# Attention stage of a one-core encoder layer: finished rows stored from SyncE, and the order of transposes, products and closings changed

## The reference, cut to what matters

```
def fox_attend(q, k, v, cq, ck, pos_q, pos_k):
    s = einsum('bqhd,bkhd->bhqk', q, k) * HEAD_DIM ** -0.5          # float32
    decay = cq[..., :, None] - ck[..., None, :]
    s = where(pos_k <= pos_q, s + decay, NEG_INF)
    p = softmax(s, axis=-1)
    return einsum('bhqk,bkhd->bqhd', p, v)
```

## Time and profile before

| | us |
|---|---|
| median of 3 runs | 2924.09 (2922.81 to 2926.6) |
| the profiled execution, its own time | 2925.41 |
| its span | 2923.8 |
| attention, from the span's start | about 640 to 1169 |
| PE busy over the span | 2766.0 (95%) |
| DVE, ACT, POOL busy | 1271.9, 895.1, 927.0 |
| mean granted TensorE clock | 0.978 |

### The profile page before, as it was taken

One profiled execution on the slowest core, in us unless ns is written; L12 is line 12 of the kernel. 1 busy time (PEld: TensorE's weight loads), 2 busy tenths in 40 slices (PEclk: granted clock), 3 DMA queues, 4 the chain that ended last, 5 costly groups with the idle time before them and its releaser, 6 DMA issues.

```text
span 2923.8 us, 40223 instructions
## 1 busy us (share of the span) xinstructions
PE 2766.0 (95%) x14550; PEld 2424.5 (83%) x14550; DVE 1271.9 (44%) x2362; ACT 895.1 (31%) x1621; POOL 927.0 (32%) x613
## 2 busy tenths in 40 slices
PE   7999999999898988799699999999999999999997
PEld 6899899987777777588599999999987888888886
DVE  4333343348786777577423223232235223222235
ACT  3201201127676766455211111212122121121122
POOL 3233334211111111444233333333245333333333
PEclk9999999999999999899899999999999999999999
DMA  6543535674433333566910111111146111111113
GB/s 180 183 125 116 159 104 157 197 186 120 104 94 93 94 93 94 164 210 208 259 57 30 57 43 43 43 43 43 43 130 197 59 44 48 53 43 56 44 43 115
DMA packets 261442, 305.23 MB, mean 104 GB/s; under 512 B 19324, under 2 KB 221704, under 8 KB 256712
## 3 DMA queue, kind: packets, MB, share of 16 engines
q1 hardware_dynamic: 209272, 256.14, 29.6%
q0 software_dynamic: 14304, 21.63, 2.9%
q10 hardware_dynamic: 37744, 25.96, 2.8%
HBM read 221.21 MB, written 82.21 MB: 104 GB/s over the span
## 4 chain that ended last, share of the span: by engine, by line
PE 46%; DMA 2%; POOL 2%; DVE 1%; ACT 0%; issue 0%; SPq 0%; POOLq 0%
PE up_bank L2340 23%; PE dn_bank L2363 23%; DMA m_x_in<-scratch_x 1%; DVE y L2294 1%; POOL y L2158 1%; DMA m_h_lo<-scratch_h_lo 0%; POOL dn_lo L2138 0%; POOL up_lo L2138 0%; DMA m_x_in<-y 0%; DMA m_raw<-in_w_down 0%; POOL u_hl L2150 0%; DVE y L2281 0%; POOL m_h_hi L2130 0%; DVE up_lo L2297 0%; ACT dn_hi L2209 0%; ACT up_hi L2209 0%
## 5 line engine op out<-in xcount | busy, mean ns | idle before, releaser
L2363 PE MATMUL dn_bank<-dn_hi,u_hl 128*128 128x512 f32 x2112 | 671.5, 390 | 6.9 <-DVE y L2279 4.4
L2150 POOL TENSOR_TENSOR u_hl<-u,u_hl 128x64 fp32r<-128x64 f32 (+2 forms) x192 | 200.2, 1066 | 900.7 <-DVE u L2266 900.7
L2363 PEld LDWEIGHTS dn_bank<-dn_hi,u_hl 128*128 128x128 f32 x2112 | 397.1, 188 | 90.7 <-DVE y L2279 4.8
L2340 PE MATMUL up_bank<-m_h_hi,up_hi 128*128 128x512 f32 (+2 forms) x1280 | 452.6, 354 | 17.1 <-DVE up_lo L2297 11.3
L2340 PE MATMUL up_bank<-m_h_lo,up_hi 128*128 128x512 f32 (+2 forms) x1280 | 451.9, 353 | 0.0
L2340 PE MATMUL up_bank<-m_h_hi,up_lo 128*128 128x512 f32 (+2 forms) x1280 | 451.9, 353 | 0.0
L2219 ACT ACTIVATE u<-up_bank 128x512 f32<-128x512 f32 (+2 forms) x160 | 83.7, 524 | 1159.8 <-PE up_bank L2340 1153.5
L2281 DVE TENSOR_TENSOR y<-dn_bank,y 128x1024 f32<-128x1024 f32 x255 | 312.0, 1224 | 289.2 <-PE dn_bank L2363 289.1
L2363 PE MATMUL dn_bank<-dn_lo,u_hl 128*128 128x512 f32 x1088 | 424.6, 390 | 0.0
L2266 DVE TENSOR_TENSOR u<-u 128x512 f32<-128x512 f32 (+2 forms) x160 | 93.9, 628 | 698.0 <-ACT u_hl L2222 698.0
L504 POOL TENSOR_TENSOR w_lo<-w_raw,w_hi 128x1024 fp32r<-128x1024 f32 x72 | 181.3, 2522 | 336.1 <-DVE w_hi L722 336.1
(11 more groups left out here) (256 smaller groups left out, 4828.0 us busy)
## 6 DMA issues: line engine op xcount, KB each, us to landing
w_raw<-in_w_in SPq DMA_DIRECT2D x72, 512.0 KB, 4.1
m_raw<-in_w_up SPq DMA_DIRECT2D x32, 1024.0 KB, 5.4
m_raw<-in_w_down SPq DMA_DIRECT2D x32, 1024.0 KB, 4.8
nck<-scratch_ncum SPq DMA_DIRECT2D x9, 1312.0 KB, 18.6
scratch_v_hl<-vhl SPq DMA_DIRECT2D x20, 512.0 KB, 2.6
q_hi<-scratch_q_hi SPq DMA_DIRECT2D x18, 528.0 KB, 7.6
q_lo<-scratch_q_lo SPq DMA_DIRECT2D x18, 528.0 KB, 9.4
v_hl<-scratch_v_hl SPq DMA_DIRECT2D x9, 1024.0 KB, 20.7
```

The lines of the kernel that those rows point to most:

```text
L2150: rest = pool.tensor_tensor(u_hl[:, o % 2, b, to], u[:, b, at], u_hl[:, o % 2, b, at].bitcast(F32), ALU.subtract)
L2340: mm = pe.matmul(up_bank[2 * (o % 2) + b][:, 0:w], wp[:, c, k, b * P:(b + 1) * P], hp[g][s][:, k, :], start=(k == 0 and p == 0), stop=(k = ...
L2363: mm = pe.matmul(bank[:, cols], u_hl[:, o % 2, b, part], wp[:, c, b, cols], start=(b == 0 and p == 0), stop=(b == 1 and p == len(passes) - 1))
```

## The change

Four things are changed, all in attention.

1. The DMA that stores finished rows leaves POOL and is issued by SP, in SP's own walk through the list. The buffer `att` is five deep instead of one, with a semaphore for each; POOL waits for the store of five closings ago, not for the one just issued. SP waits for POOL's division before each store.
2. `p_hi` and `p_lo` have four buffers instead of three (the bank that a unit is transposed into is still one of three).
3. V stands three units behind T instead of two.
4. The closing N goes in at place 2 of the next group's list instead of 4.

```
-V_BEHIND = 2
+V_BEHIND = 3
+P_BUFS = 4
+A_BUFS = 5
...
                 if late:
-                    steps.insert(4, late)
+                    steps.insert(2, late)
...
@@ sync @@
             def step(it, x):
+                if x.kind == "N":
...
+                    sp.wait_ge(att_done, upto("N", it, x.at) + 1)
+                    sp.dma_start(dst..., att[rows, x.at % A_BUFS, 0:n, :]).then_inc(att_stored[x.at % A_BUFS], 16)
                 if x.kind != "L":
                     return
...
@@ gpsimd @@
                 pool.wait_ge(n_taken, 1 + upto("N", it, x.at) + 1)
+                pool.wait_ge(att_stored[a], 16 * (per["N"] // A_BUFS * it + x.at // A_BUFS + 1))
...
-                pool.wait_ge(att_done, upto("N", it, x.at) + 1)
-                pool.dma_start(dst..., att[rows, 0:n, :]).then_inc(att_stored, 16)
-                pool.wait_ge(att_stored, 16 * (upto("N", it, x.at) + 1))
```

More of the change, by code:

```diff
@@ L1080, in __init__ @@
         self.v, self.o = v, o
-        self.at, self.free, self.exps, self.last_piece = None, None, None, None
+        self.at, self.free, self.exps, self.last_piece, self.p = None, None, None, None, None
 def attention_order():
@@ L1196, in attend @@
         sets = [sb("scores_a", [P, 4 * 1536]), sb("scores_b", [P, 4 * 2048])]
-        p_hi = sb("p_hi", [P, T_BANKS, 512], F32R)
-        p_lo = sb("p_lo", [P, T_BANKS, 512], F32R)
+        p_hi = sb("p_hi", [P, P_BUFS, 512], F32R)
+        p_lo = sb("p_lo", [P, P_BUFS, 512], F32R)
         o_t = sb("o_t", [P, 2, 512])
         o_n = sb("o_n", [P, 4, 2, HD])
-        att = sb("att", [P, 4, HD])
+        att = sb("att", [P, A_BUFS, 4, HD])
         ident_r, mask_r = pre.ident_r, pre.mask_r
@@ L1226, in attend @@
         att_done = sem("att_done")
-        att_stored = sem("att_stored")
+        att_stored = [sem(f"att_stored{i}") for i in range(A_BUFS)]
         before, body, start, per = attention_order()
+        for x in body:
+            if x.kind == "T":
+                x.p = x.at % P_BUFS
         QM = per["M"]
@@ L1265, in step @@
             def step(it, x):
+                if x.kind == "N":
+                    n = 4 if x.g < EXTRA else 1
+                    rows = slice(0, P) if x.g < EXTRA else slice(0, DEC)
+                    dst = dr["attn"][x.g * 4 * P:(x.g * 4 + n) * P, :] if n == 4 else dr["attn"][SEQ:ROWS, :]
+                    sp.wait_ge(att_done, upto("N", it, x.at) + 1)
+                    sp.dma_start(dst.rearrange("(a p) (i c) -> p a i c", a=n, c=2 * HD)[:, :, it, x.off * HD:(x.off + 1) * HD],
+                                 att[rows, x.at % A_BUFS, 0:n, :]).then_inc(att_stored[x.at % A_BUFS], 16)
                 if x.kind != "L":
@@ L1273, in step @@
                 load_values(sp, dr, h, v_hl[x.par], v_loaded[x.par])
+            for i in range(A_BUFS):
+                sp.sem_inc(att_stored[i], 16)
             loop(sp, "sync", step)
+            for i in range(A_BUFS):
+                sp.wait_ge(att_stored[i], 16 * (1 + per["N"] // A_BUFS * (HEADS // 2)))
             sp.wait_ge(qk_loaded[0], 96 * (HEADS // 2 + 1))
@@ L1323, in step @@
                     act.wait_ge(used, upto("V", it, x.at) + 1)
-                    act.activation(p_hi[:, x.at % T_BANKS, x.cols], t_bank[x.at % T_BANKS][:, x.cols], ACT.Copy).then_inc(hi_done, 1)
+                    act.activation(p_hi[:, x.p, x.cols], t_bank[x.at % T_BANKS][:, x.cols], ACT.Copy).then_inc(hi_done, 1)
                 elif x.kind == "O":
                     width = P if x.g == EXTRA else 512
-                    act.wait_ge(used, T_BANKS + upto("V", it, x.v.at) + 1)
+                    act.wait_ge(used, P_BUFS + upto("V", it, x.v.at) + 1)
                     act.wait_ge(in_rows, upto("O", it, x.at) + 1)
@@ L1367, in step @@
                     dve.wait_ge(hi_done, upto("T", it, x.at) + 1)
-                    dve.tensor_tensor(p_lo[:, x.at % T_BANKS, x.cols], t_bank[x.at % T_BANKS][:, x.cols], p_hi[:, x.at % T_BANKS, x.cols].bitcast(F32),
+                    dve.tensor_tensor(p_lo[:, x.p, x.cols], t_bank[x.at % T_BANKS][:, x.cols], p_hi[:, x.p, x.cols].bitcast(F32),
                                       ALU.subtract).then_inc(lo_done, 1)
@@ L1379, in _ @@
             pe.sem_inc(turned, 1)
-            pe.sem_inc(used, T_BANKS)
+            pe.sem_inc(used, P_BUFS)
             pe.sem_inc(in_rows, 2)
@@ L1421, in step @@
                             out, at, vb = o_bank[o % O_BANKS][:, 0:P], slice(i * P, (i + 1) * P), QT if j == CB else QT + 1 + j
-                        pe.matmul(out, v_hl[par][:, vb, :], p_hi[:, t.at % T_BANKS, at], start=x.first and i == 0, stop=False)
-                        mm = pe.matmul(out, v_hl[par][:, vb, :], p_lo[:, t.at % T_BANKS, at], start=False, stop=x.last and i == len(t.blocks) - 1)
+                        pe.matmul(out, v_hl[par][:, vb, :], p_hi[:, t.p, at], start=x.first and i == 0, stop=False)
+                        mm = pe.matmul(out, v_hl[par][:, vb, :], p_lo[:, t.p, at], start=False, stop=x.last and i == len(t.blocks) - 1)
                     mm.then_inc(used, 1)
```

12 lines of the change are left out of this document (4 added, 8 removed).

## The result

Over four runs each on one chip the kernel before took 2924.5 us and the changed one 2871.9 us: a ratio of 0.982, 95% interval 0.980 to 0.984, so 52.6 us less. The profiled execution agrees (span 2870.3 us against 2923.8), and 52.1 of the 53.5 us between them lie in attention, which is over at about 1117 us instead of 1169.

The account below looks back on a forecast made before the run. PE was taken to bound attention, busy 470.9 of 530 us. The terms 13.2 + 3.6 + 3.0 + 3.2 = 23.0 us led to 2901 us, range 2893 to 2909, or 2886 to 2918 with the clock rival and most of the slow-fetch rival.

Parts of the forecast that it names:

- The late loads, 13.2 us: At three loop returns, stores on SP delay the next head's loads, so ACT restarts 4.4 us earlier each time: 13.2 us.
- Rival (1): At the loop's return ACT's instruction fetch stays as slow; only 6.2 us of gain stay, 2918 us; chance 0.17.
- The clock at the return, 3.6 us: Behind the three loop returns, PE's clock no longer falls once the stall shrinks: 1.2 us each, 3.6 us.
- Products three behind, 3.0 us: In four second heads, more work ahead of the first product removes its 0.74 us wait: 3.0 us.
- closing forward, 3.2: In group 4 the closing moves into PE's wait ahead of the first product: 0.4 us eight times, 3.2 us.
- Where PE never waited (groups 2 and 3) nothing is gained: Step on products three behind: in groups without PE waits, the new order gains nothing.
- the 0.74: PE's wait in us at a second head's first product, expected to go with products three behind.
- the 1.0 in sum: Sign at group 4: the wait before its product is split between closing and product, about 1.0 us in sum.
- Rival (2): The clock also stays up behind group 4 in second heads, 8 us, and 5.6 more at returns: 2887 us; chance 0.15.
- only 0.74 and part of 1.38 of PE's gaps go: Argument against the clock recovering in second heads: only these parts of PE's gaps, in us, close there.
- Nobody on the path waits for POOL, so that alone is nothing.: Step on the stores in attention: removing POOL's 76.7 us of store waits gains nothing by itself.
- Rival (3): The closing holds PE for ACT's copy, 1.4 us in three groups of each head: slower, 2935 us; chance 0.04.

Follow-up runs that it names:

- experiment 5: Kernel before, POOL still storing, but SP waits for POOL's last division and issues one small spare store before its branch and loads: ratio 0.993 to the kernel before.
- experiment 6: Changed kernel with the store of the body's last closing back on POOL, the other nine on SP: ratio 0.988 to the kernel before.
- experiment 1: Kernel before with only the stores changed, issued by SP from five buffers of finished rows: ratio 0.992 to the kernel before.
- experiment 2: Kernel before with only products three units behind and four buffers of probabilities; POOL still stores: ratio 0.994 to the kernel before.
- experiment 3: Kernel before with only the closing moved, behind two steps of the next group instead of four: ratio 0.995 to the kernel before.
- experiment 9: Changed kernel with products two units behind again and three buffers of probabilities: ratio 0.986 to the kernel before.
- experiment 8: Changed kernel with the closing put back behind four steps: ratio 0.986 to the kernel before.
- experiment 4: Kernel before with products three behind, four buffers and the closing moved forward; stores stay on POOL with one buffer: ratio 0.992 to the kernel before.
- experiment 7: Kernel before with products three behind and the closing forward, POOL storing from five buffers: ratio 0.988 to the kernel before.

## Why the prediction was wrong

*The late loads, 13.2 us.* Right in mechanism and size: 13.8 of PE's waits. ACT started 4.6 us sooner behind its copy where I took 4.4 (the loads came 3.2 us behind its copy instead of the 2.1 I had, at no cost), and experiments 5 and 6 show that a later start of the loads is enough and is needed. Rival (1) fell with them. That the two sizes agree so well is in part luck: 4.4 was a choice between 3.6 and 4.8.

*The clock at the return, 3.6 us.* 4.7 measured (experiment 1): the term was a little small.

*Products three behind, 3.0 us, and closing forward, 3.2.* Here is most of the error: the order gave 22.5 us, net of the clock, instead of 6.2. Two steps failed. "Where PE never waited (groups 2 and 3) nothing is gained" took the table of waits for the whole of PE's idle time. Group 3 lost 1.2 us of gaps a head and the stretch before it 0.4; of these a wait of 0.32 (among the 40.7 us of the earlier trace rows) was listed, and nearly all of the rest is drawn as busy. And the 0.74 went to the wrong edit: with three behind alone it stays on the transposes (experiment 2), with the closing alone it goes (experiment 3). The closing's own term at group 4 was of the right kind and somewhat too large: 0.36 in first heads (experiment 3) and 0.20 in second ones (experiment 9 against 1), 2.2 against 3.2. Its wait came out near the 1.0 in sum that was foretold: 0.24 and 0.56 in first heads, 1.07 in second ones.

*Rival (2), the clock in second heads.* It carried 0.15 and was part of what happened, along with the above: the clock stayed up behind group 4 in every head, first heads too, and with POOL's part that was 9.8 us, where I had 8 for the clock alone. I argued against it that "only 0.74 and part of 1.38 of PE's gaps go". Experiment 3 removes about that and no fall is left in eight heads; experiment 2 leaves both listed waits and no fall is left either. Of the kernels with the closing behind four steps, before had six falls, experiments 1 and 5 five each, experiment 8 two, experiment 2 none; with two steps, in seven experiments and in the changed kernel, there was none. So the closing moved forward goes with no fall in 64 heads. For three behind the counts say less: experiment 8 has the same order on PE as experiment 2 and two falls, so that experiment 2 had none may be luck. The listed waits alone don't decide it; that the hidden gaps count too is likely, not shown.

*"Nobody on the path waits for POOL, so that alone is nothing."* This step failed too. The waits of the kernel before already have a line against it, which I passed over:

```profile
ACT o_n L1335 <- POOL att L1297: 3.7, 4, 1.1
```

It is one wait in each second head, where the clock had fallen as well, and the two hid each other: with the fall and without POOL T4 to G takes 17.31 us (experiment 1), with POOL and without the fall 17.73 (experiment 5), with both 17.56, with neither 15.84. So of the 9.8 us above, 2.9 lie in two first heads and are the clock's, and 6.9 lie in four second heads and come only when clock and POOL are both cured. That is most of the 7.7 us by which experiments 1 and 4 fall short of the whole. In the new order POOL costs 9.4 us at the upper clock (experiments 4 and 7); a reader who takes the order without the buffers loses them.

*Rival (3), the closing holds PE.* It did not: the closings at groups 1 and 3 list no wait.

What stays open: why the clock falls behind the same 1.4 us wait in one head and not in the next, and so whether three behind helps to keep it up at all. The counts above are over eight heads of one execution each. How three behind shortens group 3, place by place, is shown at one gap of 0.29 us and as a sum, no more.

## What to carry to other kernels

Where the ends of the bound engine's instructions are modelled, measure its idle time from start to start between milestones that both kernels have; half of this gain was in time shown as busy. When a wait is priced, price the clock behind it as well, even for gaps near 1 us: here a fall took 1.5 us, and with a few small gaps closed it no longer came. Two causes that lie on the same stretch hide each other, so the gain of one must not be read as all that it is worth. And when an order is tightened, look again at the engines that had slack in the old one, above all at one that waits for its stores to land.

## What was not expected of the hardware

At the loop's return ACT stood idle for 2.1 to 2.3 us in the runs where the next loads began 2.8 to 3.2 us behind the end of its last copy, and for 6.2 to 7.0 us in those where they had begun 1.8 us ahead of it. A delay of the loads by 4.6 to 5.0 us was the whole cure. The clock's fall behind a 1.4 us wait is not a fixed reaction: in one kernel (experiment 1) it came in five heads of eight, each time for 1.5 us.
